# Four pairs of weight tiles moved to other offsets within 512 bytes of SBUF

## What is computed

```
for l in range(2):
    mod = silu(c) @ ada_w[l] + ada_b[l]                  # shift, scale, gate for each sub-layer
    h = modulate(rmsnorm(x)); x += 0.5*(1+g1) * (silu(h @ w1) * (h @ w3)) @ w2     # 1024 -> 2816 -> 1024
    h = modulate(rmsnorm(x)); proj = h @ w_in
    ya = gelu(gate) * rg_lru(conv(rg_x))                 # 1,024 channels
    yb = stick_breaking_attention(q, k, v)               # 8 heads of 64
    yc = forgetting_attention(q, k, v, log_f)            # 8 heads of 64
    x += (1+g2) * (g[0]*(ya @ w_rg) + g[1]*(yb @ w_sb) + g[2]*(yc @ w_fox)) @ w_o
    h = modulate(rmsnorm(x)); x += 0.5*(1+g3) * swiglu(h)
return modulate(rmsnorm(x))
```

## Time and profile before

| | |
|---|---|
| median of three runs | 2769.68 us |
| the profiled execution's own time | 2768.65 us |
| its span, first to last instruction | 2766.9 us |
| granted TensorE clock, mean | 0.994 |
| TensorE (PE) busy | 2683.0 us, 97% |
| weight loads (PEld) busy | 2247.2 us |
| VectorE, ScalarE, GpSimd busy | 1288.2, 1060.9, 1163.0 us |
| HBM read, written | 319.64 MB, 2.10 MB |

### The profile page before, as it was taken

How to read it: one execution, slowest core, us unless ns; L and a number is a source line. 1 busy time by engine, 2 the same in 40 slices (tenths; PEclk the granted TensorE clock), 3 DMA queues, 4 the chain that set the end, 5 groups by cost and what they waited for, 6 DMA issues and landing times.

```text
span 2766.9 us, 31911 instructions
## 1 busy us (share of the span) xinstructions
PE 2683.0 (97%) x13172; PEld 2247.2 (81%) x13172; DVE 1288.2 (47%) x1612; ACT 1060.9 (38%) x1598; POOL 1163.0 (42%) x468
## 2 busy tenths in 40 slices
PE   3999999999999999999999999999999999999998
PEld 3888888878888878888888888888788888888887
DVE  6566337875543143511056663478545422453111
ACT  5232227654344244222252232566444442523223
POOL 2555444432223434545435554354223234345442
PEclk9999999999999999999999999999999999999999
DMA  5655533221112323523245554322112122253322
GB/s 222 213 183 198 175 123 104 89 73 61 62 61 69 99 85 130 179 95 99 96 141 189 201 190 162 102 92 89 64 61 69 62 77 95 82 189 123 102 97 76
DMA packets 90833, 323.82 MB, mean 117 GB/s; under 512 B 10048, under 2 KB 12480, under 8 KB 90432
## 3 DMA queue, kind: packets, MB, share of 16 engines
q1 hardware_dynamic: 90688, 321.78, 34.1%
HBM read 319.64 MB, written 2.10 MB: 116 GB/s over the span
## 4 chain that ended last, share of the span: by engine, by line
PE 88%; DVE 6%; ACT 4%; issue 1%; POOL 1%; DMA 0%; SPq 0%; ACTq 0%; DVEq 0%
PE bank L1277 27%; PE bank L1276 27%; PE bank L1275 27%; PE bank L1310 2%; PE bank L1426 1%; PE bank L1315 1%; DVE e_lo L1101 1%; DVE e_hi L1099 1%; PE bank L1459 1%; DVE e_f L1094 1%; POOL w_lo L448 1%; DVE ada L1175 1%; DVE gt L1001 1%; ACT w_hi L478 1%; PE bank L1473 1%
## 5 line engine op out<-in xcount | busy, mean ns | idle before, releaser
L448 POOL TENSOR_TENSOR w_lo<-raw,w_hi 128x1024 fp32r<-128x1024 f32 x440 | 1142.8, 2608 | 1491.1 <-ACT w_hi L478 1490.7
L1275 PE MATMUL bank<-h_hi,w_hi 128*128 128x512 f32 x2240 | 876.5, 391 | 9.5 <-POOL w_lo L448 9.5
L1276 PE MATMUL bank<-h_lo,w_hi 128*128 128x512 f32 x2240 | 874.2, 390 | 0.0
L1277 PE MATMUL bank<-h_hi,w_lo 128*128 128x512 f32 x2240 | 874.1, 390 | 0.0
L478 ACT ACTIVATE w_hi<-raw 128x1024 fp32r<-128x1024 f32 x440 | 464.2, 1057 | 972.9 <-PE bank L1277 901.5
L1275 PEld LDWEIGHTS bank<-h_hi,w_hi 128*128 128x128 f32 x2240 | 421.8, 188 | 98.2 <-issue 10.2
L1277 PEld LDWEIGHTS bank<-h_hi,w_lo 128*128 128x128 f32 x2240 | 421.5, 188 | 88.5
L1276 PEld LDWEIGHTS bank<-h_lo,w_hi 128*128 128x128 f32 x2240 | 421.8, 188 | 87.4
L845 DVE CUSTOM_DVE_ANT_0 ada<-ada,c_act 128x1024 f32<-128x1024 f32 x144 | 284.0, 1979 | 238.6 <-DMA ada<-ada_w 238.3
L1277 PE MATMUL bank<-g_hi,w_lo 128*128 128x512 f32 (+1 forms) x792 | 295.2, 373 | 0.0
L1276 PE MATMUL bank<-g_lo,w_hi 128*128 128x512 f32 (+1 forms) x792 | 292.3, 369 | 0.0
(11 more groups left out here) (212 smaller groups left out, 3005.6 us busy)
## 6 DMA issues: line engine op xcount, KB each, us to landing
raw<-w_units SPq DMA_DIRECT2D x440, 512.0 KB, 3.5
ada<-ada_w SPq DMA_DIRECT2D x144, 512.0 KB, 4.8
ada<-ada_w SPq DMA_DIRECT2D x8, 1024.0 KB, 16.6
x<-x_in SPq DMA_DIRECT2D x4, 512.0 KB, 6.7
wab_raw<-wab SPq DMA_DIRECT2D x2, 1024.0 KB, 5.7
y<-fin SPq DMA_DIRECT2D x8, 256.0 KB, 2.1
c_act<-c_rows SPq DMA_DIRECT2D x1, 512.0 KB, 3.8
vec<-vecs SPq DMA_DIRECT2D x3, 92.5 KB, 3.6
```

The costliest lines, as they stand in the source:

```text
L448: nc.gpsimd.tensor_tensor(w_lo[s][:, :, :], raw[u % RAW][:, :, :], w_hi[s][:, :, :].bitcast(F32), ALU.subtract).then_inc(unit_lo.sem, 1)
L1275: nc.tensor.matmul(o, wh, xh, start=start, stop=False, skip_group_check=True)
L1276: nc.tensor.matmul(o, wh, xl, start=False, stop=False, skip_group_check=True)
L1277: return nc.tensor.matmul(o, wl, xh, start=False, stop=stop, skip_group_check=True)
```

## The change

In front of each pair of weight tiles a gap is declared, so that the pair begins at a given offset from h_hi within 512 bytes: 256 for pair 0, 64 for pair 1, 32 for pair 2, 448 for pair 3. The gaps are 256, 320, 480 and 416 bytes. w_hi and w_lo of a pair now follow each other (before, the four w_hi came first). What is declared behind them, the arena too, lies 1,472 bytes further on. Nothing else changes.

```
         x = sb("x", [P, KD, T])
+        h_base = nc.sbuf_base
         h_hi = sb("h_hi", [P, KD, T], F32R)
         h_lo = sb("h_lo", [P, KD, T], F32R)
         raw = [sb(f"raw{i}", [P, UB, P]) for i in range(RAW)]
-        w_hi = [sb(f"w_hi{i}", [P, UB, P], F32R) for i in range(RING)]
-        w_lo = [sb(f"w_lo{i}", [P, UB, P], F32R) for i in range(RING)]
+        w_hi, w_lo = [], []
+        for i, shift in enumerate((256, 64, 32, 448)):
+            sb(f"w_gap{i}", [P, (shift - nc.sbuf_base + h_base) % 512 // 4])
+            w_hi.append(sb(f"w_hi{i}", [P, UB, P], F32R))
+            w_lo.append(sb(f"w_lo{i}", [P, UB, P], F32R))
         c_act = sb("c_act", [P, D])
```

## The result

The changed kernel takes 2792.08 us in the median of four runs (2790.93 to 2793.52), against 2770.18 us before: ratio 1.008, 95% interval 1.0064 to 1.0096. It is slower by 21.9 us; the forecast was 27 us slower.

The account below looks back on a forecast made before the run. TensorE, busy 97% of the span, was taken as the bound. +31.6 us on h and -4.1 on the arena, other terms 0, gave +27.5 on 2,768.65: forecast 2,797 us, 2,782 to 2,813 for this case, overall range 2,725 to 2,816.

Parts of the forecast that it names:

- Step 1, h: 6,720 matmuls of 512 columns on h: step from 226.7 to 231.4 ns, unsettled by changing offsets, +31.6 us.
- The stand-in: Forget-gate unit on h: 14 steps of 231.4 ns with an offset changing at nearly every load, taken as h's new step.
- The eight slow steps of the earlier trace: First eight h steps after a unit on ya, 231.3 ns each at offset 0, read as not yet settled.
- Step 2, the arena: 512-column matmuls on arena tiles: 2,172 in slots 0 to 2 go from 233.3 to 231.4 ns, -4.1 us; slot 3 nothing.
- Step 3, 256 columns: 1,152 short matmuls on h and 720 on the arena: offset makes no difference, 0; +9 us at most.
- Step 4, the splits: ScalarE writing w_hi and GpSimd writing w_lo, 440 of each: any slower write stays hidden, 0.
- That the offset does nothing: Rival for all matmuls: the 6.6 ns between h and g has another source, time stays at 2,770 us; chance 0.07.
- rule of two independent read ports: Skill's rule on SBUF reads: loading weights takes nothing from the running matmul, so no offset matters and the sum is 0.
- The 215.7 ns for 512 columns: Skill's figure for one matmul, used to estimate what is left to gain on h: 74 us.
- The period of 64: Rival on weight offsets: only 64 bytes matter, so slots 0, 1 and 3 equal 0; +9.0 us, 2,779 us; chance 0.08.
- New offsets that rest lower than the old: Rival on each matmul's stall: faster, 2,755 or 2,738 us, floor 2,637; chance 0.42, of which 0.12 by over 1.6%.
- Turns worse than any row: Rival on h: alternating offsets keep matmuls near 235.0 ns, +56 us, 2,825 us; chance 0.07 for over 2,816.

Follow-up runs that it names:

- run without turns: Changed kernel with each FFN pair issued as two whole units, one after the other: 2779.71 us, ratio 1.0035 to the kernel before.
- uniform 64: Changed kernel with all four weight pairs 64 bytes from h and the arena back at 352 from h: 2800.03 us, ratio 1.0114 to the kernel before.
- all-zero kernel: Changed kernel with all weight tiles and the arena at offset 0 from h within 512 bytes: 2750.35 us, ratio 0.9941 to the kernel before.
- run with the arena's move undone: Changed kernel, weight offsets kept, with the arena back at 352 bytes from h: 2794.55 us, ratio 1.0092 to the kernel before.

## Why the prediction was right

**Step 1, h.** The step was forecast at 231.4 ns and is 231.4 in the mean. The term was +31.6 and is +27.9 us, mostly because the base was not 226.7 but 227.1 (2.6 us): the slow steps after each change of tile were in the time before already. The other 1.1 us are steps over 245 ns, which became shorter. The path, TensorE's own steps, and the sign were right; the reason was right for the smaller part. In the pairs the matmuls do stay unsettled (231.9 in the mean of the four slots, 230.4 in slot 0 where whole units rest at 226.7). In the single units they do settle, each slot at its own value: 227.6, 233.2, 233.3 and 229.3 ns. And the run without turns keeps a mean of 230.65: of the 4.3 ns, 3.5 are resting values and 0.8 the turns, where the prediction had put all of it on matmuls that do not settle.

That both came to 231.4 is luck in part. The stand-in was the forget-gate unit, in which the prediction saw an offset that changes at nearly every load. With a period of 256, wf_hi and wf_lo stand at the same offset, which changes only with k: 96, 128, 160, 192, 224. Steps that rest at once at the values of the table above would mean 232.5 ns there, an estimate, so its 231.4 is no sign of unsettled steps. The eight slow steps of the earlier trace rows are: over the 26 changes from arena to h in the kernel before, the first eight steps on h mean 231.4 ns (225 to 236 by place), and from the ninth on 226.7.

**Step 2, the arena.** -4.1 forecast, -3.9 measured, but the agreement is luck: slots 0, 1 and 3 stayed at 233.2, and slot 2, which got the offset 256, fell to 228.1. Not three slots at 231.4, but one at nearly the old value of h.

**Step 3, 256 columns.** Forecast 0, measured -2.6 us. The rows at 0 and at 160 are alike, and I took from that that offsets do not matter for short matmuls. The uniform 64 shows that they do, by 6.7 ns in the other direction: two offsets were too few.

**Step 4, the splits.** ScalarE's mean went from 1,057 to 1,058 ns and GpSimd's from 2,608 to 2,626; hidden, as said.

**The rivals.** That the offset does nothing is refuted by the all-zero kernel and the uniform 64. The Trainium skill's rule of two independent read ports (page "TensorE: Matmul & The Clock Gate", section "Step-by-step: what each phase is for") does not hold as a statement on time here, in the sense in which the prediction used it, that no offset could matter: with nothing changed but the weights' address, 512-column steps went from 226.7 to 233.3 ns. Whether the two streams meet at a port, a bank or elsewhere, no run here shows. The 215.7 ns for 512 columns, which the prediction quotes from the section "Back-to-back issue gap", stand on the same page of the Trainium skill in the section named here; the lowest mean of 512-column steps in any run is 226.7. The period of 64 is refuted, as 64 and 192 differ from 0; the period is 256, which the prediction had not listed, and which makes slot 0 free. New offsets that rest lower than the old: on h none of the offsets tried does for 512 columns; on the arena one slot of the four did, since 256 is as good as 0. Turns worse than any row: slot 1, the worst in the pairs, comes to 233.8, not 235.

## What to carry to other kernels

Where TensorE is the bound, take the step between starts from the timeline for each pair of stationary and moving tile, and compare it with the offset of their addresses within 256 bytes. In this kernel a 512-column float32r stream is best, of all offsets tried, with both at the same offset, and the 160 bytes that small tiles had pushed the arena off cost 20 us, which one gap gave back. A declared tile of odd size ahead of the large ones changes all offsets behind it, so a layout change is also a change of matmul time. The best offset depends on the matmul's length, so measure with the lengths at hand.

## What the hardware did that I had not expected

- A period of 256 bytes: 0 and 256 are the same (226.7 ns), and 4 bytes off costs 5.5 ns a step.
- 256-column matmuls prefer another offset: 113.3 ns at 64 against 120.0 at 0, while 512-column ones lose 6.6 ns there.
- The offset of 192 rests at 229.1 to 229.5 ns in whole units, and 8 bytes at 230.7; all others but 0 are at 232.3 or above. On the arena in the run with the arena's move undone 192 came to 231.3, which no run explains.
- The step depends on what ran before: after a change from arena to h, eight matmuls mean 231.4 ns at an offset at which the next ones take 226.7.
- A load at another offset slows the matmuls around it that have the good one: with w_lo alone at 64, the two products that read w_hi took 229.3 and 228.6 ns, against 227.2 before. But a mix of 160 and 224 on the arena took 231.2 ns, less than either alone (233.5 and 233.2).
- The 13.4 ns over the columns' own time that are left at offset 0 have no explanation from these runs.
